# The last two expert blocks of a mixture of experts: rows returned through HBM against rows returned by products with slot matrices

## The chip, the cores and the metric

One core of one Trainium2 chip. The metric is the device time of one execution in microseconds (us), lower is better. The engines named are TensorE (PE), VectorE (DVE), ScalarE (ACT), GpSimd (POOL) and SyncE (SP), which issues transfers.

## The reference, cut to what matters

Two network blocks run over 256 tokens of 1024 elements in float32. The first has two layers of feed-forward and mixer stages, the second a recurrent and attention mixer and then a mixture of 16 experts with two experts for each token. Only the end of the second is touched:

```python
combine = einsum('nk,nke->ne', w_sel, one_hot(e_id, 16))   # two weights for each token
for e in range(16):
    he = silu(hf @ w1[e]) * (hf @ w3[e])                   # 1024 -> 512
    y = y + combine[:, e:e + 1] * (he @ w2[e])             # 512 -> 1024
x = x + g2[:, None, :] * y
```

## The kernel before

All weights are streamed from HBM in units of 128x2048 float32 (1 MB). Each unit is split into a high part by ScalarE (line 982) and a low part by VectorE (line 1346), and a product is made from three float32r products. In the expert stage each token is given two slots, one for each of its experts. A block is 128 slots of one expert. There are 19 blocks, 16 and three more for experts with over 128 tokens. A block takes six units: four for the two input products (`product`, lines 791 to 793) and two for the output product (`outputs`, lines 820 to 822). The order in which TensorE works in round b is: the first half of block b's input products, the transposes of block b - 1's hidden rows (`turn_hidden`, line 802), the second half of the input products, the output products of block b - 1. Gathers of the slots of the next pair of blocks (`gather`, line 775) lie between them; they use one-hot matrices that POOL makes (`one_hot`, lines 553 and 556).

Each engine has its own queue, written out by hand, and waits on semaphores. Of a block's output rows ScalarE evicts the left 512 columns from bank 3 (line 1041, semaphore `y_left`) and VectorE the right 512 from bank 4, multiplied by the gain in `mod` (line 1504, semaphore `y_right`). The output products of a block wait for both evictions of the block before it, and for hTlo (line 1484), which VectorE makes after ScalarE's hThi (line 1028). The rows go to `ybuf`, which is the tile that the profile names lnrow, and POOL stores them in the HBM tensor `yd` (`store`, line 564). After block 18 POOL waits for the last two stores and issues four indirect reads (line 577): for each half of the tokens (i) and each choice (j), 128 rows of 4 KB from `yd` to `raw`. ScalarE weights the first choice (line 1046), VectorE adds the second, weighted (line 1510), multiplies the left half by the gain (line 1514) and adds the sum to x (line 1516). SP sends four pieces of x out (line 506).

The 1 MB tiles for loaded units are six: three thirds of `raw`, two parts of `mod`, and `raw5`. SP loads the next unit into a tile when the low split of the unit in it is done.

Of the kernel before, what the change touches and what calls it, by code (L numbers as in the profile page):

```python
# [68 lines left out]
D_EXPERT = 512  # L69
V_SC, V_RC, V_RCB, V_BM, V_RGB, V_A, NVEC = 0, 3, 7, 8, 10, 12, 13  # L70
# [108 lines left out]
def build(nc, t, out):  # L179
    ctx = ExitStack()  # L180
    with ctx:
# [48 lines left out]
        def xT_banks(i):  # L230
# [103 lines left out]
        tests = sb("tests", [P, 2, BATCH], F32, moe)  # L334
        oneh = sb("oneh", [P, 2, TT, BATCH], F32R, moe)
# [76 lines left out]
            "hT_ps y_left y_right first_w final").split()}  # L412
# [69 lines left out]
        def sp_block2(sp):  # L482
            for p in range(6 * BLOCKS):
                b, j = UNIT_OF[p]
                if p < RING:
                    sp.wait_ge(lo_done, UNITS - (UNITS - 1 - p) % RING + RING)
                elif p == 3:
                    sp.wait_ge(ev["h1_free"], 1)
                elif p == 4:
                    sp.wait_ge(x_done, 4 * N_H2 + 4)  # L490
                elif p >= RAWS:
                    unit_split(sp, p - RAWS)
                if p == 0:
                    expert = 0
                elif j == 0:
                    if b == 1:
                        sp.wait_ge(ev["emap"], 1)
                    expert, last = sp.value_load(emap[0:1, b:b + 1], min_val=0, max_val=EXPERTS - 1), expert
                e = expert if j < 4 or b == BLOCKS - 1 else last
                src = t["experts"][bass.ds(e * 6 + j, 1), :, :]  # L500
                sp.dma_start(raws[p % RAWS], src.rearrange("o p n -> p (o n)")).then_inc(expert_loaded(p)[0], 16)
            for i in range(TT):
                for half in range(2):
                    cs = slice(512 * half, 512 * half + 512)
                    sp.wait_ge(ev["final"], 2 * i + half + 1)
                    sp.dma_start(out[0, i * P:(i + 1) * P, cs], x[:, i, cs]).then_inc(out_done, 16)
            sp.wait_ge(out_done, 16 * 2 * TT)

        def pool_block2(pool):
# [55 lines left out]

            pool.wait_ge(ev["slots"], 1)
            one_hot(1)
            one_hot(2)
            for b in range(BLOCKS):
                if b % 2 == 1 and b // 2 + 3 < BATCHES:  # L570
                    one_hot(b // 2 + 3)
                store(b)
            for b in (BLOCKS - 2, BLOCKS - 1):
                pool.wait_ge(stored[b % 2], stored_to(b))
            for i in range(TT):
                for j in range(2):
                    pool.indirect_dma_start(raw[:, i, j * D:(j + 1) * D], None, t["yd"],
                                            bass.IndirectOffsetOnAxis(slot_i[:, i, j:j + 1], 0)).then_inc(back[i], 16)

        def pe_block2(pe, cols_unit, tokens_unit, rows_unit, transpose_x, open_sums):  # L580
# [243 lines left out]

            for group in range(8):
                gather(0, group)
            for b in range(BLOCKS + 1):
                nxt = b // 2 + 1
                groups = [4 * (b % 2) + n for n in range(4)] if nxt < BATCHES else []
                if b < BLOCKS:  # L830
# [6 lines left out]
                    product(b, 1)  # L837
                if b >= 1:
                    turn_hidden(b - 1)
# [7 lines left out]
                if b >= 1:  # L847
                    outputs(b - 1, 4)
                    outputs(b - 1, 5)

        def act_block2(act, turn, split_xT, silu, hid_hi):
# [162 lines left out]
            for b in range(BLOCKS + 1):  # L1014
                nxt = b // 2 + 1
                pairs = [2 * (b % 2) + n for n in range(2)] if nxt < BATCHES else []
                if b < BLOCKS:
# [5 lines left out]
                    freed(b, 1)  # L1023
                if b >= 1:
# [11 lines left out]
                if b >= 1:  # L1036
# [6 lines left out]
            act.wait_ge(ev["weighed"], 1)  # L1043
            for i in range(TT):
                act.wait_ge(back[i], 32)
                act_fn(lnrow[:, i, :], raw[:, i, 0:D], ACT.Identity, scale=rt[:, i, 33:34]).then_inc(ev["first_w"], 1)

        def dve_block2(dve, pieces, turn, split_xT, hid_lo, refine):
# [388 lines left out]
            v.tensor_copy(slot_i[:, :, :], slot[:, :, :]).then_inc(ev["slots"], 1)  # L1437
# [37 lines left out]

            for b in range(BLOCKS + 1):
                nxt = b // 2 + 1
                pairs = [2 * (b % 2) + n for n in range(2)] if nxt < BATCHES else []
                if b < BLOCKS:
                    freed(b, 0)  # L1480
                    freed(b, 1)
                if b >= 1:
# [4 lines left out]
                if b < BLOCKS:  # L1487
# [9 lines left out]
                    for pair in pairs[1:]:  # L1497
                        select(nxt, pair)
                if b >= 1:
                    freed(b - 1, 4)  # L1500
                    dve.wait_ge(*expert_used(expert_unit(b - 1, 5) + 1))
                    if b >= 3:
                        dve.wait_ge(stored[(b - 1) % 2], stored_to(b - 3))
                    v.tensor_tensor(ybuf[:, (b - 1) % 2, 512:], bank(4), row(mod, 5)[:, 512:], ALU.mult).then_inc(ev["y_right"], 1)
                    freed(b - 1, 5)
            for i in range(TT):
                dve.wait_ge(ev["first_w"], i + 1)
                for half in range(2):
                    cs = slice(512 * half, 512 * half + 512)
                    v.scalar_tensor_tensor(lnrow[:, i, cs], raw[:, i, D + 512 * half:D + 512 * half + 512], rt[:, i, 34:35],  # L1510
                                           lnrow[:, i, cs], ALU.mult, ALU.add)
                    dve.drain()
                    if half == 0:
                        v.tensor_tensor(lnrow[:, i, cs], lnrow[:, i, cs], row(mod, 5)[:, cs], ALU.mult)
                        dve.drain()
                    v.tensor_tensor(x[:, i, cs], x[:, i, cs], lnrow[:, i, cs], ALU.add).then_inc(ev["final"], 1)
# [678 lines left out]
```

## Time and profile before

| | |
|---|---|
| median of 3 runs | 1994.21 us (1993.26 to 1995.16) |
| the profiled execution | 1990.22 us, span 1988.5 us |
| busy share of the span | TensorE 92%, its weight loads 85%, VectorE 70%, ScalarE 48%, POOL 8% |
| mean granted TensorE clock | 0.958 of 2.4 GHz |
| expert stage | from about 1593 us to the end; a round takes 18.7 us |

The span runs from the first to the last instruction. The busy shares are averages over all stages; the end of the span, after TensorE's last product, has to be read by itself. The chain of waits is followed back from the last instruction. In a timeline, the brackets hold how long the engine was idle before the instruction and which instruction released it.

### The profile page before, as it was taken

How to read it: one execution, taken by the hardware profiler on the slowest of the kernel's cores; microseconds unless marked ns; L12 is line 12 of the kernel's file. 1: busy time of each engine (PE TensorE's matmuls, PEld its weight loads, DVE VectorE, ACT ScalarE, POOL GpSimd, SP SyncE). 2: the span in 40 equal slices, each digit the busy share in tenths (PEclk: the TensorE clock that was granted, in tenths of full speed). 3: DMA queues.
4: the chain of work that ended last, by engine and by line, in shares of the span. 5: the costliest groups of instructions: out<-in, count | busy, mean ns of one | idle time of the engine just before them, and what ended most of it. 6: DMA issues, size and time to landing. Idle time of an engine off the chain costs nothing.

```text
span 1988.5 us, 31309 instructions
## 1 busy us (share of the span) xinstructions
PE 1830.8 (92%) x12367; PEld 1691.0 (85%) x12367; DVE 1383.9 (70%) x1417; ACT 951.6 (48%) x870; POOL 162.9 (8%) x153
## 2 busy tenths in 40 slices
PE   7999899998999899989999899988996489999995
PEld 7999799997999799979999799967984378888884
DVE  6444686856766644467785676675787678988885
ACT  4343466534433444436563433443344257777773
POOL 1000000000000000000000000010000043424401
PEclk9999899999999899989999999998997789999998
DMA  6555355653866455544556476743340279999993
GB/s 237 190 190 190 128 200 181 220 184 142 290 245 243 157 181 181 187 157 171 180 202 221 148 261 248 270 152 135 108 149 1 72 281 360 357 367 361 364 367 134
DMA packets 61893, 418.10 MB, mean 210 GB/s; under 512 B 7312, under 2 KB 7680, under 8 KB 13936
## 3 DMA queue, kind: packets, MB, share of 16 engines
q1 hardware_dynamic: 51392, 369.19, 51.8%
q0 software_dynamic: 10400, 47.73, 6.9%
q8 instruction: 58, 0.95, 0.2%
q14 instruction: 27, 0.22, 0.0%
q10 hardware_dynamic: 16, 0.01, 0.0%
HBM read 405.88 MB, written 11.02 MB: 210 GB/s over the span
## 4 chain that ended last, share of the span: by engine, by line
PE 85%; DVE 6%; issue 4%; DVEq 3%; DMA 1%; POOL 1%; POOLq 1%; ACT 0%; ACTq 0%
PE ps L1599 16%; PE ps L1600 16%; PE ps L1601 16%; PE ps L1626 5%; PE ps L1627 5%; PE ps L1630 4%; PE ps L792 3%; PE ps L791 3%; PE ps L793 3%; PE ps L820 2%; PE ps L775 2%; PE ps L821 2%; PE ps L822 2%; PE ps L1612 1%; PE ps L1613 1%
## 5 line engine op out<-in xcount | busy, mean ns | idle before, releaser
L1884 DVE TENSOR_TENSOR wlo<-raw,whi 128x2048 fp32r<-128x2048 f32 x236 | 538.1, 2291 | 343.6 <-ACT whi L1733 340.8
L1599 PE MATMUL ps<-xThi,whi 128*128 128x256 f32 x2400 | 684.9, 285 | 10.9 <-DVE xTlo L1895 8.3
L1600 PE MATMUL ps<-xTlo,whi 128*128 128x256 f32 x2400 | 683.4, 285 | 0.0
L1601 PE MATMUL ps<-xThi,wlo 128*128 128x256 f32 x2400 | 683.1, 285 | 0.0
L1733 ACT ACTIVATE whi<-raw 128x2048 fp32r<-128x2048 f32 x236 | 449.9, 1910 | 370.4 <-PE ps L1601 270.0
L1599 PEld LDWEIGHTS ps<-xThi,whi 128*128 128x128 f32 x2400 | 465.0, 194 | 15.2 <-issue 11.3
L1600 PEld LDWEIGHTS ps<-xTlo,whi 128*128 128x128 f32 x2400 | 465.0, 194 | 1.8 <-issue 0.2
L1601 PEld LDWEIGHTS ps<-xThi,wlo 128*128 128x128 f32 x2400 | 465.0, 194 | 0.0
L1346 DVE TENSOR_TENSOR wlo<-raw,whi 128x2048 fp32r<-128x2048 f32 x76 | 176.4, 2330 | 24.8 <-ACT whi L982 24.8
L982 ACT ACTIVATE whi<-raw 128x2048 fp32r<-128x2048 f32 x76 | 145.6, 1918 | 49.8 <-PE ps L793 27.4
L1627 PE MATMUL ps<-wlo,hhi 128*128 128x512 f32 x352 | 137.5, 391 | 0.0
L1626 PE MATMUL ps<-whi,hhi 128*128 128x512 f32 x352 | 137.4, 390 | 0.0
L791 PE MATMUL ps<-whi,xsel_hi 128*128 128x512 f32 x304 | 120.2, 395 | 0.8 <-ACT xsel_hi L1010 0.8
L792 PE MATMUL ps<-wlo,xsel_hi 128*128 128x512 f32 x304 | 120.2, 395 | 0.0
L793 PE MATMUL ps<-whi,xsel_lo 128*128 128x512 f32 x304 | 119.5, 393 | 0.0
L1630 PE MATMUL ps<-whi,hlo 128*128 128x512 f32 x352 | 108.5, 389 | 0.0
L1750 ACT ACTIVATE sil<-ps 128x512 f32<-128x512 f32 x44 | 26.3, 598 | 160.0 <-PE ps L1601 160.0
L1346 DVE TENSOR_TENSOR wlo<-mod,whi 128x2048 fp32r<-128x2048 f32 x38 | 88.2, 2320 | 18.9 <-ACT whi L982 18.9
L553 POOL TENSOR_SCALAR tests<-iota,slot 128x256 f32<-128x256 f32 (+1 forms) x36 | 83.1, 2310 | 49.5 <-DVE slot_i L1437 46.3
L982 ACT ACTIVATE whi<-mod 128x2048 fp32r<-128x2048 f32 x38 | 72.7, 1913 | 17.7 <-PE ps L793 17.7
L1950 DVE SCALAR_TENSOR_TENSOR mod<-adaraw,csil_now,mod 128x512 f32 (+1 forms) x96 | 72.2, 752 | 12.1 <-issue 6.5
L1630 PEld LDWEIGHTS ps<-whi,hlo 128*128 128x128 f32 x352 | 66.1, 188 | 14.1
(433 smaller groups left out, 2650.5 us busy)
## 6 DMA issues: line engine op xcount, KB each, us to landing
raw<-stream SPq DMA_DIRECT2D x236, 1024.0 KB, 4.9
raw<-experts SPq DMA_DIRECT2D x76, 1024.0 KB, 7.7
mod<-experts SPq DMA_DIRECT2D x38, 1024.0 KB, 7.2
adaraw<-ada POOLq DMA_DIRECT2D x24, 1024.0 KB, 5.2
yd<-lnrow POOLq DMA_DIRECT2D x19, 512.0 KB, 8.6
lnrow<-ln_g POOLq DMA_DIRECT2D x6, 512.0 KB, 5.1
lnrow<-ln_b POOLq DMA_DIRECT2D x6, 512.0 KB, 6.3
x_sb<-x SPq DMA_DIRECT2D x1, 1024.0 KB, 5.8
```

Of the source, the lines that this page charges most:

```text
L791: mm(o, h, wh[:, rs], start=k == 0, stop=False)
L792: mm(o, h, wl[:, rs], start=False, stop=False)
L982: act_fn(splits[p % SPLITS][0], raws[p % RAWS], ACT.Copy).then_inc(hi_done, 1)
L1346: v.tensor_tensor(splits[p % SPLITS][1], raws[p % RAWS], splits[p % SPLITS][0].bitcast(F32), ALU.subtract).then_inc(lo_done, 1)
L1599: nc.tensor.matmul(outs[tile], wh, xh[:, k, :], start=k == 0, stop=False)
L1600: nc.tensor.matmul(outs[tile], wh, xl[:, k, :], start=False, stop=False)
L1601: last = nc.tensor.matmul(outs[tile], wl, xh[:, k, :], start=False, stop=k == KD - 1)
L1626: nc.tensor.matmul(o, h, whi[:, slot, c:c + 512], start=start and k == 0, stop=False)
L1627: nc.tensor.matmul(o, h, wlo[:, slot, c:c + 512], start=False, stop=False)
L1630: last = nc.tensor.matmul(bank(4 + 2 * i + n), lo, whi[:, slot, c:c + 512], start=False, stop=stop and k == 1)
L1733: act_fn(whi[:, slot, :], raw[:, slot, :], ACT.Copy).then_inc(hi_done, 1)
L1884: v.tensor_tensor(wlo[:, slot, :], raw[:, slot, :], whi[:, slot, :].bitcast(F32), ALU.subtract).then_inc(lo_done, 1)
```

## The change

The last two blocks (17 and 18, `FAR` = 17) are no longer stored. For them VectorE builds, in round 17, matrices that hold for each token its weight at its slot (`far_shares`). TensorE transposes them in round 18 (`turn_shares`), ScalarE copies them to `share`, and after the last output product TensorE multiplies them with the rows in `ybuf` (`far_products`: four float32 products of 512 columns for each of the two blocks, in four banks). The left halves of these blocks' rows are multiplied by the gain on VectorE: block 17's in place, block 18's at its eviction. VectorE then adds the four banks to x.

The blocks 0 to 16 are stored and read as before, but the reads follow block 16's store on POOL, and the low split of unit 109, which frees the tile. A token whose slot is in the last two blocks reads a row of zeros that POOL writes ahead (`slot_i` is bounded to that row). ScalarE weights the first choice in round 18, ahead of the eviction of block 17's left half. VectorE does three of the four sums (`near_sum`) before it evicts block 18 and the fourth after it. The sums build up in the third part of `raw`.

```diff
+FAR = BLOCKS - 2
+FAR_SLOT = FAR * SLOTS
+FAR_BANKS = [5, 6, 7, 0]
...
# POOL
+            g.memset(tests[0:1, :, :], 0.0)
+            pool.drain()
+            for half in range(2):
+                pool.dma_start(t["yd"][FAR_SLOT:FAR_SLOT + 1, 512 * half:512 * half + 512],
+                               tests[0:1, :, :].rearrange("p a s -> p (a s)")).then_inc(ev["zero_row"], 16)
+            pool.wait_ge(ev["zero_row"], 32)
             pool.wait_ge(ev["slots"], 1)
...
-                store(b)
-            for b in (BLOCKS - 2, BLOCKS - 1):
+                if b < FAR:
+                    store(b)
+            unit_split(pool, expert_unit(BLOCKS - 1, 3))
+            for b in (FAR - 2, FAR - 1):
                 pool.wait_ge(stored[b % 2], stored_to(b))
...
# TensorE
+            def turn_shares():
+                pe.wait_ge(ev["shares_in"], 1)
+                for n in range(2):
+                    for i in range(TT):
+                        last = nc.tensor.transpose(bank(5, (2 * n + i) * P, (2 * n + i + 1) * P),
+                                                   tests[:, i, n * SLOTS:(n + 1) * SLOTS], eye[:, :])
+                last.then_inc(ev["shareT_ps"], 1)
+
+            def far_products(b):
+                n = b - FAR
+                for half in range(2):
+                    pe.wait_ge(ev["y_right"], FAR + 2 + (1 + half if n else 0))
+                    for i in range(TT):
+                        ins = mm(bank(FAR_BANKS[2 * half + i]), share[:, n, i, :], ybuf[:, b % 2, 512 * half:512 * half + 512],
+                                 start=n == 0, stop=n == 1)
+                        if n == 1:
+                            ins.then_inc(ev["far_ps"], 1)
...
                     product(b, 1)
+                    if b == BLOCKS - 1:
+                        turn_shares()
...
+            pe.wait_ge(ev["shareT"], 1)
+            far_products(FAR)
+            far_products(FAR + 1)
...
# ScalarE
                     freed(b, 1)
+                    if b == BLOCKS - 1:
+                        act.wait_ge(ev["shareT_ps"], 1)
+                        act_fn(share[:, :, :, :].rearrange("p n i s -> p (n i s)"), bank(5), ACT.Copy).then_inc(ev["shareT"], 1)
...
-                if b >= 1:
+                if b == BLOCKS - 1:
+                    act.wait_ge(ev["weighed"], 1)
+                    unit_split(act, expert_unit(FAR, 4))
+                    for i in range(TT):
+                        act.wait_ge(back[i], 32)
+                        act_fn(raw[:, 2, i * D:(i + 1) * D], raw[:, i, 0:D], ACT.Identity,
+                               scale=rt[:, i, 33:34]).then_inc(ev["first_w"], 1)
+                if 1 <= b < BLOCKS:
                     freed(b - 1, 4)
...
# VectorE
-            v.tensor_copy(slot_i[:, :, :], slot[:, :, :]).then_inc(ev["slots"], 1)
+            v.tensor_scalar(far[:, :, :], slot[:, :, :], float(FAR_SLOT), None, ALU.subtract)
+            v.tensor_scalar(slot_i[:, :, :], slot[:, :, :], float(FAR_SLOT), None, ALU.min).then_inc(ev["slots"], 1)
...
+            def far_shares():
+                dve.wait_ge(ev["oneh"], BATCHES - 1)
+                other = share[:, :, :, :].rearrange("p n i s -> p n (i s)")
+                for i in range(TT):
+                    v.tensor_scalar(tests[:, i, :], iota[:, :], far[:, i, 0:1], rt[:, i, 33:34], ALU.is_equal, ALU.mult)
+                    v.tensor_scalar(other[:, i, :], iota[:, :], far[:, i, 1:2], rt[:, i, 34:35], ALU.is_equal, ALU.mult)
+                dve.drain()
+                for i in range(TT):
+                    ins = v.tensor_tensor(tests[:, i, :], tests[:, i, :], other[:, i, :], ALU.add)
+                ins.then_inc(ev["shares_in"], 1)
...
+                if b == FAR:
+                    far_shares()
                 if b >= 1:
                     dve.wait_ge(hhi_done, FFN_DONE + b)
...
+                if b == BLOCKS:
+                    dve.wait_ge(ev["y_left"], FAR + 1)
+                    v.tensor_tensor(ybuf[:, FAR % 2, 0:512], ybuf[:, FAR % 2, 0:512], row(mod, 5)[:, 0:512],
+                                    ALU.mult).then_inc(ev["y_right"], 1)
+                    near_sum(0, 0)
+                    near_sum(0, 1)
+                    near_sum(1, 1)
                 if b >= 1:
...
+                    if b == BLOCKS:
+                        v.tensor_tensor(ybuf[:, (b - 1) % 2, 0:512], bank(3), row(mod, 5)[:, 0:512], ALU.mult).then_inc(
+                            ev["y_right"], 1)
                     v.tensor_tensor(ybuf[:, (b - 1) % 2, 512:], bank(4), row(mod, 5)[:, 512:], ALU.mult).then_inc(ev["y_right"], 1)
...
+            near_sum(1, 0)
+            dve.drain()
+            for half in range(2):
+                cs = slice(512 * half, 512 * half + 512)
+                for i in range(TT):
+                    n = 2 * half + i
+                    dve.wait_ge(ev["far_ps"], n + 1)
+                    v.tensor_tensor(x[:, i, cs], x[:, i, cs], bank(FAR_BANKS[n]), ALU.add).then_inc(ev["final"], 1)
```

`near_sum(i, half)` is the body of VectorE's closing loop in the kernel before, with the sums in `raw[:, 2]` in place of lnrow and without the signal to SP. SP's output transfers now go left halves first.

## Rows read from the trace of the kernel before

**Rows 1.** The page, part 1: busy time of TensorE and the others.
```profile
PE 1830.8 (92%) x12367; PEld 1691.0 (85%) x12367; DVE 1383.9 (70%) x1417; ACT 951.6 (48%) x870; POOL 162.9 (8%) x153
```

**Rows 2.** The chain that ended last, 1958 to the end: start, duration, what.
```profile
1959.22 0.70 DVE hTlo L1484
1960.01 0.47 PE ps L820
...
1965.51 0.24 PE ps L822
...
1967.01 2.90 DMA yd<-lnrow
...
1970.74 1.04 POOL raw L577
1972.08 5.40 DMA raw<-yd,slot_i
1977.57 1.16 ACT lnrow L1046
...
1985.40 0.69 DVE x_sb L1516
```

**Rows 3.** Timeline of TensorE, modulation stage: start, duration, line, form, count.
```profile
1332.64 3.60 PE L586 MATMUL ps<-mod,ones 128*128 128x512 f32 x8
```

**Rows 4.** Timeline of VectorE, 1932 to the end.
```profile
1932.72 0.68 DVE L1484 TENSOR_TENSOR hTlo<-ps,hThi 128x512 fp32r<-128x512 f32 x1
...
1939.13 0.42 DVE L1459 CAST xsel_lo<-ps 128x256 fp32r<-128x256 f32 x1
...
1943.72 4.55 DVE L1346 TENSOR_TENSOR wlo<-raw,whi 128x2048 fp32r<-128x2048 f32 x2 [0.32 <-ACT whi L982]
...
1978.75 0.75 DVE L1510 SCALAR_TENSOR_TENSOR lnrow<-raw,rt,lnrow 128x512 f32<-128x512 f32 x1 [12.28 <-ACT lnrow L1046]
...
1980.96 0.75 DVE L1510 SCALAR_TENSOR_TENSOR lnrow<-raw,rt,lnrow 128x512 f32<-128x512 f32 x1
...
1982.39 0.74 DVE L1510 SCALAR_TENSOR_TENSOR lnrow<-raw,rt,lnrow 128x512 f32<-128x512 f32 x1
```

**Rows 5.** Groups by form of VectorE, from 1560: busy time, mean ns, idle before.
```profile
L1439 DVE TENSOR_SCALAR mod<-iota,slot 128x256 f32<-128x256 f32 x2 | 0.8, 456 | 0.0
```

**Rows 6.** Timeline of TensorE, rounds 17 and 18.
```profile
1935.49 0.45 PE L820 MATMUL ps<-whi,hThi 128*128 128x512 f32 x1
...
1941.01 0.39 PE L791 MATMUL ps<-whi,xsel_hi 128*128 128x512 f32 x1
...
1946.51 0.60 PE L802 MATMUL ps<-eye,mod 128*128 128x128 f32 x4
```

**Rows 7.** Timeline of ScalarE, round 18: eviction of block 17's left half.
```profile
1958.10 0.60 ACT L1041 ACTIVATE lnrow<-ps 128x512 f32<-128x512 f32 x1 [3.52 <-PE ps L822]
```

**Rows 8.** DMA issues of 1940 to 1945 and of 1900 to 1990, us to landing.
```profile
yd<-lnrow POOLq DMA_DIRECT2D x1, 512.0 KB, 4.0
...
raw<-yd,slot_i POOLq DMA_INDIRECT x4, 5.4
```

**Rows 9.** Timeline of POOL, the last stores and the last read.
```profile
1943.94 0.53 POOL L564 DMA_DIRECT2D yd<-lnrow  x1 [18.17 <-DVE lnrow L1504]
...
1967.01 0.53 POOL L564 DMA_DIRECT2D yd<-lnrow  x1 [7.14 <-DVE lnrow L1504]
...
1974.61 0.94 POOL L577 DMA_INDIRECT raw<-yd,slot_i  x1 [0.30 <-issue]
```

**Rows 10.** Instructions on the tile tests, POOL: shortest, median, longest in ns.
```profile
L553 POOL TENSOR_SCALAR tests<-iota,slot x36: 1137/2432/5103, 1591.4 to 1880.9; 128x256 f32<-128x256 f32 x32, 128x128 f32<-128x128 f32 x4
```

**Rows 11.** Timeline of TensorE, round 1: the gathers that wait for POOL.
```profile
1611.21 1.22 PE L775 MATMUL ps<-oneh,xThi 128*128 128x256 f32 x4 [4.98 <-POOL oneh L556]
```

**Rows 12.** Stretches of 1 us: busy of each engine, granted clock (PEclk), DMA share.
```profile
1609.00:1610.00 1.00, 0.00 (x0) 0.00 (x0) 1.00 (x1) 0.14 (x1) 1.00 (x1) 0.54 1.25 377
...
1615.00:1616.00 1.00, 1.00 (x3) 0.78 (x3) 0.00 (x0) 0.00 (x0) 0.85 (x2) 0.55 1.18 238
```

More of the change, by code:

```diff
@@ L334, in build @@
         tests = sb("tests", [P, 2, BATCH], F32, moe)
+        far = sb("far", [P, TT, 2], F32, moe)
+        share = sb("share", [P, 2, TT, SLOTS], F32, moe)
         oneh = sb("oneh", [P, 2, TT, BATCH], F32R, moe)
@@ L411, in build @@
             "tables_in h2_hi h2_lo picked rank_ps emap slots weighed oneh0 oneh "
-            "hT_ps y_left y_right first_w final").split()}
+            "hT_ps y_left y_right first_w final zero_row shares_in shareT_ps shareT far_ps").split()}
         out_done = sem("out_done")
@@ L501, in sp_block2 @@
                 sp.dma_start(raws[p % RAWS], src.rearrange("o p n -> p (o n)")).then_inc(expert_loaded(p)[0], 16)
-            for i in range(TT):
-                for half in range(2):
+            for half in range(2):
+                for i in range(TT):
                     cs = slice(512 * half, 512 * half + 512)
-                    sp.wait_ge(ev["final"], 2 * i + half + 1)
+                    sp.wait_ge(ev["final"], 2 * half + i + 1)
                     sp.dma_start(out[0, i * P:(i + 1) * P, cs], x[:, i, cs]).then_inc(out_done, 16)
@@ L576, in pool_block2 @@
                 for j in range(2):
[L577 removed]
+                    pool.indirect_dma_start(raw[:, i, j * D:(j + 1) * D], None, t["yd"][0:FAR_SLOT + 1, :],
                                             bass.IndirectOffsetOnAxis(slot_i[:, i, j:j + 1], 0)).then_inc(back[i], 16)
@@ L1042, in act_block2 @@
                     freed(b - 1, 5)
[L1043 to L1046, printed above, removed]
         def dve_block2(dve, pieces, turn, split_xT, hid_lo, refine):
@@ L1474, in dve_block2, with near_sum @@
             v.tensor_tensor(R(33, 35), R(33, 35), R(3, 4).to_broadcast([P, TT, 2]), ALU.mult).then_inc(ev["weighed"], 1)
+            def far_shares():
[8 more added lines that the diff above has]
+                ins.then_inc(ev["shares_in"], 1)
+            def near_sum(i, half):
+                dve.wait_ge(ev["first_w"], i + 1)
+                cs = slice(512 * half, 512 * half + 512)
+                acc = raw[:, 2, i * D + 512 * half:i * D + 512 * half + 512]
+                v.scalar_tensor_tensor(acc, raw[:, i, D + 512 * half:D + 512 * half + 512], rt[:, i, 34:35], acc,
+                                       ALU.mult, ALU.add)
+                dve.drain()
+                if half == 0:
+                    v.tensor_tensor(acc, acc, row(mod, 5)[:, cs], ALU.mult)
+                    dve.drain()
+                v.tensor_tensor(x[:, i, cs], x[:, i, cs], acc, ALU.add)
             for b in range(BLOCKS + 1):
@@ L1503, in dve_block2 @@
                         dve.wait_ge(stored[(b - 1) % 2], stored_to(b - 3))
+                    if b == BLOCKS:
+                        v.tensor_tensor(ybuf[:, (b - 1) % 2, 0:512], bank(3), row(mod, 5)[:, 0:512], ALU.mult).then_inc(
+                            ev["y_right"], 1)
                     v.tensor_tensor(ybuf[:, (b - 1) % 2, 512:], bank(4), row(mod, 5)[:, 512:], ALU.mult).then_inc(ev["y_right"], 1)
                     freed(b - 1, 5)
[L1506 to L1516, printed above, removed]
+            near_sum(1, 0)
+            dve.drain()
+            for half in range(2):
+                cs = slice(512 * half, 512 * half + 512)
+                for i in range(TT):
+                    n = 2 * half + i
+                    dve.wait_ge(ev["far_ps"], n + 1)
+                    v.tensor_tensor(x[:, i, cs], x[:, i, cs], bank(FAR_BANKS[n]), ALU.add).then_inc(ev["final"], 1)
         def proj_bank(name, a):
```

## The prediction

> **What bounds the kernel now.** I read the page first: TensorE is busy for 92% of the span [rows 1], so only what shortens its stream or the stretches without it can pay. Then the chain of waits, in its last stretch [rows 2]. TensorE's last product of the last expert block starts at 1965.51 us and ends at about 1965.74. From there to the end of the span, at 1988.5, TensorE does nothing: 22.8 us. The chain in that tail is serial: eviction, store of block 18 to HBM (2.90 us), the first two of four indirect reads (issued from 1970.74, landed at 1972.08 + 5.40 = 1977.48), ScalarE's weighting of 1.16 us at 1977.57, VectorE's sums until 1986.09, then the output transfer. The reader is to see that every link waits for the one ahead, and that no engine is busy twice. The change works on this tail. The question is what it puts in its place and what it pushes into the stream in front.
>
> **The new tail, from the end T of the last product.** TensorE goes on with eight products of a float32 share matrix and a block's rows. The nearest rows are the four float32 products of 512 columns in the modulation stage: 8 records (two for each product) in 3.60 us, the first seven of them 3.0 us apart, so 0.43 us a record and 0.86 us a product [rows 3]. Four for block 17 need only rows that are there; four for block 18 need VectorE's two evictions, ready 1.4 us after T, inside the first four. So TensorE sets the pace: 8 x 0.86 = 6.9 us, 0.2 us for the last one's drain through the array and the semaphore, and the last addition starts at T + 7.1. In the kernel before, the last addition starts at 1985.40 and the span ends at 1988.5, 3.1 us later, and that part stays [rows 2]. Since the next product can start some 0.1 us before the modelled end of the last, the new tail is 10.1 us. Saved: 22.8 - 10.1 = 12.7 us. At half clock the eight products would take 13.7 us; I exclude that for the likeliest case, as TensorE comes straight from 24 products.
>
> VectorE's own work must not come later. In its last round it now does one gain product, and three of the four sums, beside the last 24 products. Its rows are 2.21 us for a sum with the gain (1978.75 to 1980.96) and 1.43 us without (to 1982.39) [rows 4], with 0.6 for the gain product 5.7 us in all. The 24 products take 1960.01 to 1965.74, 5.7 us [rows 2]. That just fits. The fourth sum, 2.2 us, lies under the share products. Only when the reads land late do these three come late, and the same wait then holds TensorE, below.
>
> **What is added ahead, on VectorE.** The share matrices are built in round 17 between the weight splits and the product hTlo of block 16: four compares of 128x256 and two additions. The nearest row is the compare at 0.456 us [rows 5]; overlapped, some 0.4 each, 2.4 us in all. hTlo starts at 1932.72 [rows 4] and would now end at 1935.8; TensorE wants it at 1935.49 [rows 6]. That costs 0.4 to 0.5 us. The queue behind it is also later: the selection at 1939.13 [rows 4] comes some 2 us later, to 1941.5, where TensorE wants it at 1941.01 [rows 6] (0.5 later by now). Together 0.6 us; bounds 0 (all in VectorE's gaps) and 2.4. Two splits later VectorE is back in step. The loads that SP issues behind these splits move by up to 2 us, and their landings lie 5 us ahead of use.
>
> **On TensorE** four transposes go between the products of block 18. The same form, four of them, stands at 1946.51: the four records span 0.60 us, of which the last's drain of some 0.2 us overlaps the next product [rows 6]. I take 0.4; the bounds are 0.3 and 0.6. So the end of block 17's outputs moves from 1957.9 to 1958.9, and with the transposes of block 18's hidden rows TensorE has nothing to do from 1959.3.
>
> **On ScalarE** the copy of the shares, 0.6 us, lies in its gap: it idles for 3.52 us before 1958.10 [rows 7]. Removed are the stores of blocks 17 and 18 (POOL's queue, 0.5 us each, nobody waited for the first). The row of zeros is written by POOL while it waits for the slots; the extra small instruction ahead of the slots' semaphore delays POOL and the first gathers by some 0.1 us (below the 0.46 us of the wide compare, as it has 4 columns).
>
> **The moved reads and the new wait.** POOL issues the reads after the store of block 16. That store is issued at 1943.94 and lands after 4.0 us [rows 8, 9]; with VectorE's eviction about 0.9 later (the delay above, less the gap before it), it lands at 1948.9. POOL then takes 0.8 to 1.1 us to wake, so the first read is issued at 1950.0. Loads of weights are over by then. In the kernel before, the four were issued from 1970.74 to 1974.61, each landing 4.2 to 5.5 us after its issue, the median 5.4 [rows 2, 8, 9]; so the first pair is in after 6.7 us and the second after 9.3. Moved: 1956.7 and 1959.3.
>
> Who waits? ScalarE, whose queue now has the two weightings before the eviction of block 17's left half. Behind that stands hThi of block 18, then VectorE's hTlo, then TensorE's last 24 products, which need all of them. In the kernel before the chain is eviction 1958.10 [rows 7], hThi 0.5 later, hTlo 1959.22, product 1960.01 [rows 2]. Now the second weighting starts at 1959.4 and takes 1.15, the eviction starts at 1960.6, hThi at 1961.1, hTlo at 1961.7, and the products at 1962.5. Without the reads they would start at 1961.0. The reads cost 1.5 us.
>
> Sum: 12.7 saved, less 0.6, 0.4, 0.1 and 1.5, gives 10.1 us. The profiled execution took 1990.22 us at a span of 1988.5; the median of the runs shown is 4 us (0.2%) above it. 1994.2 - 10.1 = **1984.1 us**. About 0.2%, 4 us, is what a measurement can tell from no change.
>
> **Reads that start beside VectorE's splits.** In the kernel before the reads ran with VectorE idle. Now they are issued beside VectorE's last three splits, some 2.3 us each (the two from 1943.72 took 4.55 [rows 4]). What POOL does beside such splits is seen in two rows: its compares take 1.14 us at best and 2.43 us at the median, 5.10 at most [rows 10]; but its plain transfer, issued at 1943.94 inside a double split, took 0.53 us, as it did at 1967.01 with VectorE idle [rows 9]. The read is nearer to the second, so I take no delay; the other end is 1.3 us for each of four reads.
>
> On this, the Trainium skill speaks against the change: SBUF — State Buffer holds, under the shared port pair, that a GpSimd instruction which reads SBUF and a VectorE instruction with two SBUF inputs exclude each other, and that descriptors of transfers issued from GpSimd starve when it is locked out. The compares agree with that rule and the plain transfer does not show it; by it the result would be that of the second rival.
>
> **Rivals.**
> First, **the reads are hidden**: they need to land by 1957.9, 1.5 us earlier than worked out. For it: the store alone took 2.90 us [rows 2], and 1.1 of its 4.0 is the load beside it. Against: that load moves later too. It gives 1982.6, and with the share matrices fully in VectorE's gaps 1982.0.
>
> Second, **POOL held off by the splits**: 1.3 us for each read, 5.2 in all. TensorE's products start at 1967.7, after 8.4 us of idleness. The clock then matters: before 1611.21 TensorE had idled 4.98 us [rows 11], the granted clock had fallen to half (1.2 GHz) in the stretch from 1609, and it was back at full (2.4 GHz) only in that from 1615 [rows 12], 4.3 us of work later; half of this, 2.2 us, is lost. Sum: 10.1 - 5.2 - 2.2 = 2.7 us, 1991.5. A partial delay of 1 to 3 us gives 1985 to 1987.
>
> Third, **slower, by the same queue**: the decision is in one landing. If each read is held as long as POOL's longest compare (5.10 instead of 1.14), the second pair lands 16 us late, at 1975; the products start at 1978, and with the clock the saving turns into 10.1 - 16 - 2.2 = -8.1 us, 2002. It decides from a landing 8 us later than worked out (10.1 less the clock's 2.2), 1967.3. Against it: VectorE has only three splits left, 7 us of work, so more than 7 us of delay by it isn't to be had.
>
> Fourth, **no change that can be told**: the tail is shortened, but the share products run at half clock and the round ahead takes 2.4 us instead of 0.6: 10.1 - 6.8 - 1.8 = 1.5 us, 1992.7. Needs a long stall in front, so it joins the second.
>
> **How the numbers follow.** Likeliest case (stall of 0 to 3 us more or less as worked out): 0.55. Hidden: 0.18. Held off by about the second rival's price: 0.19 (half of it within 4 us of before). No change otherwise: 0.05. Slower: 0.03. Faster by over 0.2%: 0.55 + 0.18 + 0.09 + 0.01 = 0.83; same 0.13; slower 0.04. The range: low end the hidden case less 1.6 us for VectorE's splits or the first gathers falling more luckily (POOL's one-hot there holds TensorE 4.98 us [rows 11]), 1980.5; the high end is short of the second rival's full price, 1990.5.
>
> **What will show it.** In the tail eight float32 products of 0.86 us, the last addition about 7 us after the last expert product, and the end some 10 us after it. TensorE's idle time before the last 24 products, 1.5 us before, should be 3.2, released through hTlo. ScalarE's two weightings should lie at 1956.8 and 1959.5, each released by the read. In round 17 TensorE should wait less than 1 us for VectorE. POOL's read instructions should stay near 1 us; if they take 2 or more, the second rival holds. The prediction is wrong if the reads land after 1962 or if the granted clock falls before the last 24 products.

## The result, and the profile after

The changed kernel takes 1979.8 us (median of 4, 1978.66 to 1980.68) against 1994.33 us (median of 4); the ratio is 0.993 with a 95% interval of [0.9917, 0.9942]. It is faster, as forecast (1984.1 us), but 14.5 us less where 10.1 were forecast, and 0.7 us outside the stated range. The two profiled executions differ less: 1990.22 us before and 1980.68 after, 9.5 us. Two numbers that differ this much need a clock of their own, so I first measure both traces from one event that lies ahead of everything that the change touches in the expert stage, TensorE's first gather. Timelines of TensorE, after:

```profile
1594.92 1.23 PE L790 MATMUL ps<-oneh,xThi 128*128 128x256 f32 x4 [4.55 <-DVE oneh L1489]
...
1602.42 0.47 PE L806 MATMUL ps<-whi,xsel_hi 128*128 128x512 f32 x1 [0.83 <-ACT xsel_hi L1050]
```

Before, the same gather starts at 1593.00 us. From there to the end of the span it is 1988.5 - 1593.0 = 395.5 us before and 1979.0 - 1594.9 = 384.1 us after. So the change is worth **11.4 us** behind the first gather, and the changed kernel's profiled execution was 1.9 us later on arriving there. The reader is also to see what is missing in the rows: the next wait of the kernel before, 4.98 us for POOL's one-hot matrix [rows 11], is not there any more. POOL's timeline, after, shows why:

```profile
1547.06 0.51 POOL L573 MEMSET tests<- 1x512 f32 x1
1559.18 1.01 POOL L576 DMA_DIRECT2D yd<-tests  x2 [11.60 <-issue]
1593.55 2.47 POOL L559 TENSOR_SCALAR tests<-iota,slot 128x256 f32<-128x256 f32 x2 [33.35 <-DVE slot_i L1484]
1596.34 0.72 POOL L562 TENSOR_TENSOR oneh<-tests 128x256 fp32r<-128x256 f32 x1 [0.32 <-issue]
```

and the same place before:

```profile
1591.37 2.58 POOL L553 TENSOR_SCALAR tests<-iota,slot 128x256 f32<-128x256 f32 x2 [46.30 <-DVE slot_i L1437]
1600.01 0.72 POOL L556 TENSOR_TENSOR oneh<-tests 128x256 fp32r<-128x256 f32 x1 [6.05 <-issue]
```

Before, POOL stood still for 6.05 us between its compares and its first addition, and nothing that the profile names ended it ("issue"). After, that pause is 0.32 us, and a long one (11.60 us) stands behind the memset of the row of zeros, in a stretch in which POOL waits for the slots anyway.

At the other end, the chain that ended last, after:

```profile
1951.89 5.80 DMA raw<-yd,slot_i
...
1957.71 0.02 ACT raw L1084
...
1957.89 1.45 ACTq L185
1959.34 0.50 ACT hThi L1071
...
1959.86 0.70 DVE hTlo L1560
...
1960.65 0.76 PE ps L835
...
1968.69 0.23 PE ps L837
1968.93 6.88 PE ps L855 x16
...
1975.83 0.69 DVE x_sb L1599
```

It answers to [rows 2]. The serial tail of store, reads and sums is gone: behind the last expert product come the eight share products (16 records, 6.88 us) and one addition. But the chain now reaches TensorE's last 24 products through the fourth read, ScalarE's weighting and the eviction behind it. TensorE, after:

```profile
1954.61 0.60 PE L817 MATMUL ps<-eye,mod 128*128 128x128 f32 x4
1960.65 0.76 PE L835 MATMUL ps<-whi,hThi 128*128 128x512 f32 x1 [5.45 <-DVE hTlo L1560]
...
1965.48 0.63 PE L837 MATMUL ps<-whi,hTlo 128*128 128x512 f32 x1
...
1968.53 0.40 PE L837 MATMUL ps<-whi,hTlo 128*128 128x512 f32 x1
```

It idles 5.45 us, where the kernel before idled 1.5, and the first half of the 24 products takes 0.63 us for each record instead of 0.40. The granted clock in stretches (PEclk, the third number from the end) says the same:

```profile
1956.00:1958.00 2.00, 0.00 (x0) 0.00 (x0) 0.00 (x0) 0.29 (x1) 0.00 (x0) 1.00 0.46 188
1958.00:1960.00 2.00, 0.00 (x0) 0.00 (x0) 0.14 (x1) 1.83 (x3) 0.00 (x0) 0.80 0.00 0
1960.00:1962.00 2.00, 1.35 (x3) 1.16 (x4) 1.93 (x4) 0.00 (x0) 0.00 (x0) 0.50 0.00 0
...
1966.00:1968.00 2.00, 2.00 (x10) 1.65 (x9) 0.21 (x1) 0.00 (x0) 0.00 (x0) 0.99 0.00 0
```

It fell to half (1.2 GHz) within 1958 to 1960, while TensorE waited, and was back at 2.4 GHz by 1966. Why the reads came late is seen in two timelines, POOL's and VectorE's, after:

```profile
1944.95 1.03 POOL L592 DMA_INDIRECT raw<-yd,slot_i  x1 [4.14 <-DVE wlo L1392]
1946.29 2.18 POOL L592 DMA_INDIRECT raw<-yd,slot_i  x1 [0.30 <-issue]
1948.78 2.81 POOL L592 DMA_INDIRECT raw<-yd,slot_i  x1 [0.31 <-issue]
1951.89 2.50 POOL L592 DMA_INDIRECT raw<-yd,slot_i  x1 [0.30 <-issue]
```

```profile
1945.33 2.29 DVE L1392 TENSOR_TENSOR wlo<-mod,whi 128x2048 fp32r<-128x2048 f32 x1 [0.94 <-ACT whi L1022]
...
1948.48 2.29 DVE L1392 TENSOR_TENSOR wlo<-mod,whi 128x2048 fp32r<-128x2048 f32 x1 [0.26 <-ACT whi L1022]
...
1951.29 2.28 DVE L1392 TENSOR_TENSOR wlo<-raw,whi 128x2048 fp32r<-128x2048 f32 x1
```

The first read was issued in VectorE's gap before a split and took 1.03 us. Each of the other three meets a split. The splits end at 1947.62, 1950.77 and 1953.57; the reads end at 1948.47, 1951.59 and 1954.39, each 0.82 to 0.85 us behind a split's end. That is a read that starts its work only when the split is over. The Trainium skill (SBUF — State Buffer, Who interferes with whom) states such a mutual exclusion of a VectorE instruction with two SBUF inputs and a GpSimd instruction that reads SBUF. This trace agrees for the reads that began under a split, 2.18 to 2.81 us for 1.03. It does not show the reverse: the split that began under the first read took its usual 2.29 us.

The account, position by position on both traces:

```
                                      before     after    after - before
first gather starts                  1593.00   1594.92    +1.92
transposes of block 0's hidden rows  1626.37   1620.92    -5.45   = 1.92 - 7.37 (POOL's pause)
transposes of block 16's hidden rows 1927.81   1923.55    -4.26   = -5.45 + 1.19 (rounds 2 to 17)
transposes of block 18's hidden rows 1957.90   1954.61    -3.29   = -4.26 + 0.97 (rounds 17, 18)
last 24 products start               1960.01   1960.65    +0.64   = -3.29 + 3.93 (reads)
last of them starts                  1965.35   1968.53    +3.18   = +0.64 + 2.54 (half clock)
end of the span                      1988.5    1979.0     -9.5    = +3.18 - 12.7 (tail)
```

The 7.37 us lie between the first gather and the transposes of round 1: 33.4 us before and 26.0 us after. In the changed kernel without the drain, below, it is 33.5 us again, so the 7.37 us are the pause and the half clock behind it. The 1.19 us that are lost later belong to no step of the change that I can name. The 24 output products of a round take 5.59 us where they took 5.47. Two lines of the profile between 1640 and 1900 us show it, the output products of hThi before and after (shortest, median and longest in ns):

```profile
L820 PE MATMUL ps<-whi,hThi x107: 389/389/404, 1653.0 to 1899.5; 128*128 128x512 f32 x107
```

```profile
L835 PE MATMUL ps<-whi,hThi x112: 393/396/396, 1647.7 to 1898.5; 128*128 128x512 f32 x112
```

That makes two rounds 37.84 us long where they were 37.70, at full granted clock in both. All profiles of the changed kernel and its variants have it, the one without the memset and the drain too; the kernel before with a drain does not. Why it is so stays open: no run varied it.

Of the 0.97 us in rounds 17 and 18, by TensorE's timelines, 0.15 is the wait for hTlo, 0.07 lies ahead of the share transposes, 0.43 is these, and two times 0.16 are the slower output products again.

### The profile page after: what moved, and what is told of

Read it like the earlier page. It is cut to its first block, busy times and chain, and to the rows that moved or that the text cites. A ratio compares the mean times of both kernels' runs of the same rounds, so it can differ in the third digit from the quotient of the medians.

```text
span 1979.0 us, 31365 instructions
## 1 busy us (share of the span) xinstructions
PE 1843.0 (93%) x12387; PEld 1696.8 (86%) x12387; DVE 1388.8 (70%) x1430; ACT 950.9 (48%) x870; POOL 171.5 (9%) x154
## 4 chain that ended last, share of the span: by engine, by line
PE 86%; DVE 7%; DVEq 3%; issue 1%; ACT 1%; DMA 1%; POOL 1%; POOLq 0%; ACTq 0%
PE ps L1682 16%; PE ps L1684 16%; PE ps L1683 16%; PE ps L1709 5%; PE ps L1710 5%; PE ps L1713 5%; PE ps L806 3%; PE ps L807 3%; PE ps L808 3%; PE ps L790 2%; PE ps L835 2%; PE ps L836 2%; PE ps L837 2%; PE ps L1695 1%; PE ps L1696 1%
## 5 line engine op out<-in xcount | busy, mean ns | idle before, releaser
L559 POOL TENSOR_SCALAR tests<-iota,slot 128x256 f32<-128x256 f32 (+1 forms) x36 | 82.8, 2302 | 37.7 <-DVE slot_i L1484 33.4
L1664 POOL DMA_DIRECT2D adaraw<-ada x24 | 12.7, 528 | 794.8 <-DVE tick L2036 441.4
```

## The experiments

Eight variants ran beside the changed kernel, and the kernel before once more. Each is timed against the kernel before on the same chip; the column "from the gather" is the span's end less the start of the first gather in the run's profile.

```
                    median us  ratio [95%]               from the gather
changed kernel        1979.8   0.993  [0.9917, 0.9942]   384.1
POOL memset + drain   1985.0   0.9956 [0.9939, 0.9973]   387.7
POOL drain only       1985.14  0.996  [0.9948, 0.9972]   388.4
no memset, no drain   1988.86  0.9982 [0.9969, 0.9995]   391.4
late weightings       1974.65  0.9908 [0.9891, 0.9924]   377.8
reads wait            1986.73  0.9963 [0.9951, 0.9976]   388.9
plain reads           1975.31  0.9914 [0.9896, 0.9932]   377.7
splits from PSUM      1976.85  0.9906 [0.9888, 0.9925]   380.5
early share products  1972.25  0.9902 [0.9883, 0.992]    376.4
before, once more     1987.41  (one execution)           395.4
```

The last column has a scatter of its own of up to 0.7 us. In the first gather TensorE works at half clock for a while, and in the profiles of "POOL memset + drain" and "early share products" the granted clock came back 1 to 2 us sooner than in the others. By the transposes of round 1 these two were at 25.4 and 25.3 us from the gather, the drain alone and the changed kernel at 26.0. Smaller differences between two rows are to be read position by position. The ratios of the late weightings, the plain reads, the splits from PSUM and the early share products have overlapping intervals, so their times alone do not put these four in an order.

### POOL's pause

**Memset and drain in the kernel before.**

```diff
+            g.memset(tests[0:1, :, :], 0.0)
+            pool.drain()
             pool.wait_ge(ev["slots"], 1)
```

> The kernel before with one memset of 2 KB and one drain on POOL ahead of its wait for the slots, and nothing else of the change. Theory (a pause that POOL takes once, at its first computing instructions of the stage, is moved under an idle stretch): POOL's idle time of 6.05 us before its first addition goes to under 0.5 us, TensorE's wait of 4.98 us for the one-hot matrix and the half clock behind it are gone, 5 to 6.5 us saved, about 1988.5 us. Rival (the pause differs from execution to execution, or the gain of the changed kernel in this stretch comes from its transfers of zeros): no change, 1994.3 us.

Measured: 7.8 us less from the gather. POOL's timeline:

```profile
1592.79 2.48 POOL L553 TENSOR_SCALAR tests<-iota,slot 128x256 f32<-128x256 f32 x2 [46.62 <-DVE slot_i L1439]
1595.42 0.73 POOL L556 TENSOR_TENSOR oneh<-tests 128x256 fp32r<-128x256 f32 x1 [0.15 <-issue]
```

The pause is 0.15 us and TensorE's wait for POOL is gone from its list of waits. Two instructions that compute nothing of use are worth more than half of what the whole change brought.

**The changed kernel without them.** The zeros come from a tile that is zero already.

```diff
-            g.memset(tests[0:1, :, :], 0.0)
-            pool.drain()
-            for half in range(2):
-                pool.dma_start(t["yd"][FAR_SLOT:FAR_SLOT + 1, 512 * half:512 * half + 512], ...)
-            pool.wait_ge(ev["zero_row"], 32)
+            pool.dma_start(t["yd"][FAR_SLOT:FAR_SLOT + 1, :].rearrange("o (p n) -> (o p) n", n=P),
+                           zero_w[0:KD, :].bitcast(F32)).then_inc(ev["zero_row"], 16)
+            pool.wait_ge(ev["zero_row"], 16)
```

> The changed kernel with the row of zeros taken from a tile that is zero already, so without the memset and the drain on POOL. Theory of the pause: it is back ahead of POOL's first addition, TensorE waits about 5 us for the one-hot matrix, 1985 to 1986 us. Rival (the transfers, or a few instructions more or less in POOL's stream, moved the pause): as the changed kernel, 1979.8 us.

Measured: the pause is back with nearly the length of before, and TensorE waits for it (POOL, then TensorE):

```profile
1602.64 0.73 POOL L562 TENSOR_TENSOR oneh<-tests 128x256 fp32r<-128x256 f32 x1 [6.13 <-issue]
```

```profile
1613.85 1.22 PE L787 MATMUL ps<-oneh,xThi 128*128 128x256 f32 x4 [5.16 <-POOL oneh L562]
```

From the gather it is 391.4 us, 7.3 more than the changed kernel. The transfers of zeros are not what moved the pause.

**The drain alone, in the kernel before.**

```diff
+            pool.drain()
             pool.wait_ge(ev["slots"], 1)
```

> The kernel before with one drain on POOL ahead of its wait for the slots, and no memset. If POOL's pause belongs to its first drain behind a row of transfers, it is taken under the idle stretch: no pause ahead of the first addition, 7 us less than before, about 1986 us. If it belongs to its first computing instruction, the pause stays, 1993 us.

Measured: 388.4 us from the gather, 7.1 less than before, and again 0.15 us ahead of the first addition. So the pause belongs to POOL's first drain behind its row of transfers, not to its first computing instruction.

### The reads

**The reads held until the last split is done.**

```diff
-            unit_split(pool, expert_unit(BLOCKS - 1, 3))
+            unit_split(pool, expert_unit(BLOCKS - 1, 5))
```

> The changed kernel with POOL's four reads held until the last low split (unit 113) is done. Theory (the reads take 2.2 to 2.8 us each because VectorE's splits shut POOL out): each read now takes 1.0 us, from 1953.7 us; the second pair lands at 1963.5 instead of 1957.7, TensorE idles 11 us, and the end comes 6 us later, about 1986 us. Rival (they are slow through the transfers under way or through their number): the reads still take 2.2 to 2.8 us each, the second pair lands at 1968 to 1969, the end comes 11 us later, about 1991 us.

Measured: the reads behind the last split, POOL's timeline:

```profile
1956.20 1.03 POOL L592 DMA_INDIRECT raw<-yd,slot_i  x1 [13.04 <-DVE wlo L1392]
1957.54 0.98 POOL L592 DMA_INDIRECT raw<-yd,slot_i  x1 [0.30 <-issue]
1958.82 0.94 POOL L592 DMA_INDIRECT raw<-yd,slot_i  x1 [0.30 <-issue]
1960.06 0.94 POOL L592 DMA_INDIRECT raw<-yd,slot_i  x1 [0.31 <-issue]
```

Full speed, as in the kernel before. TensorE idles 11.44 us before its last 24 products, 6.0 us more than in the changed kernel. The end comes only 4.8 us later (6 forecast), because the clock came back sooner: the 24 products took 7.0 us instead of 8.1. The rival, that they are slow by their number, is out; what else ran in that stretch is still open.

**Plain transfers in place of the gather by slot.** The gather by slot is left out: fixed rows of the same size are read.

```diff
-                    pool.indirect_dma_start(raw[:, i, j * D:(j + 1) * D], None, t["yd"][0:FAR_SLOT + 1, :],
-                                            bass.IndirectOffsetOnAxis(slot_i[:, i, j:j + 1], 0)).then_inc(back[i], 16)
+                    pool.dma_start(raw[:, i, j * D:(j + 1) * D],
+                                   t["yd"][(2 * i + j) * SLOTS:(2 * i + j + 1) * SLOTS, :]).then_inc(back[i], 16)
```

> The changed kernel with its four indirect reads replaced by plain transfers of 128 rows each from the same HBM tensor, issued by POOL at the same place (the gather by slot is left out). Theory (an indirect read has to read its column of indices in SBUF and is shut out by VectorE's two-input splits, a plain transfer isn't): 0.53 us for each, the second pair lands by 1951.5, TensorE waits 1.5 us before its last 24 products, full clock, about 1973.5 us. Rival (everything that POOL issues there is held): 2 to 3 us for each transfer, as the changed kernel, 1979.8 us.

Measured, POOL and VectorE:

```profile
1947.57 2.09 POOL L592 DMA_DIRECT2D raw<-yd  x4 [3.76 <-DVE wlo L1392]
```

```profile
1948.34 2.29 DVE L1392 TENSOR_TENSOR wlo<-mod,whi 128x2048 fp32r<-128x2048 f32 x1 [0.94 <-ACT whi L1022]
```

Four in 2.09 us, though a split began at 1948.34 and lay over the last two of them. TensorE idles 1.5 us, the end is at 377.7 us from the gather. A plain transfer isn't held, an indirect one is. So the starving of descriptors that the prediction named beside the exclusion is not seen here. (The landing forecast was too early: ScalarE's second weighting started at 1956.18 on a released read, 6.5 us behind the end of the issues; it no longer held anybody.)

**The last three splits with one SBUF operand.** VectorE's split of units 111 to 113 takes its first operand from PSUM. The true low parts of these three units are left out.

```diff
+                if p >= expert_unit(FAR, 5):
+                    v.tensor_tensor(splits[p % SPLITS][1].rearrange("p (a n) -> p a n", a=4),
+                                    bank(6).unsqueeze(1).to_broadcast([P, 4, 512]),
+                                    splits[p % SPLITS][0].bitcast(F32).rearrange("p (a n) -> p a n", a=4),
+                                    ALU.subtract).then_inc(lo_done, 1)
+                    return
                 v.tensor_tensor(splits[p % SPLITS][1], raws[p % RAWS], splits[p % SPLITS][0].bitcast(F32),
                                 ALU.subtract).then_inc(lo_done, 1)
```

> The changed kernel, with VectorE's last three low splits (units 111 to 113) taking their first operand from a PSUM bank instead of the SBUF tile raw: same shape and engine, one SBUF operand instead of two (these three units' low parts are left out of the result). Theory (POOL's reads are shut out by a VectorE instruction with two SBUF operands, whatever else runs): the splits still take about 2.3 us, the four reads take 0.94 to 1.04 us each, the second pair lands 5.4 us after its issue, TensorE waits 1.5 us before its last 24 products and runs at full clock, about 6.3 us less than the changed kernel, from the first gather to the end 377.8 us instead of 384.1. Rival (a busy VectorE, or the other work of that stretch, slows the reads): they still take 2.2 to 2.8 us, 384.1 us.

Measured, VectorE and POOL:

```profile
1947.66 2.29 DVE L1393 TENSOR_TENSOR wlo<-ps,whi 128x2048 fp32r<-128x2048 f32 x1 [0.94 <-ACT whi L1022]
```

```profile
1947.22 1.03 POOL L592 DMA_INDIRECT raw<-yd,slot_i  x1 [4.08 <-DVE wlo L1398]
1948.56 0.98 POOL L592 DMA_INDIRECT raw<-yd,slot_i  x1 [0.31 <-issue]
1949.84 0.94 POOL L592 DMA_INDIRECT raw<-yd,slot_i  x1 [0.30 <-issue]
1951.09 0.94 POOL L592 DMA_INDIRECT raw<-yd,slot_i  x1 [0.31 <-issue]
```

VectorE is exactly as busy as before, the reads take 0.94 to 1.03 us. Of the four reads two lie wholly inside a split. That settles the cause: it is the second SBUF operand of the split. The time, however, was not what I expected. TensorE idled 2.7 us and not 1.5, because ScalarE's second weighting, released at 1957.30, still stands ahead of the eviction (the prediction had this right, with 3.2). And the clock fell although TensorE had been at work again for more than 1 us (stretches of 1 us; PEclk is the third number from the end):

```profile
1960.00:1961.00 1.00, 0.76 (x3) 0.68 (x4) 1.00 (x3) 0.00 (x0) 0.00 (x0) 1.00 0.00 0
1961.00:1962.00 1.00, 1.00 (x5) 0.80 (x4) 0.93 (x2) 0.00 (x0) 0.00 (x0) 0.78 0.06 16
1962.00:1963.00 1.00, 1.00 (x4) 0.81 (x3) 0.93 (x3) 0.00 (x0) 0.00 (x0) 0.50 0.00 0
```

So 3.6 us came back, from the gather, of the 6.3 expected.

**The weightings moved behind hThi.** On ScalarE they no longer stand ahead of the eviction.

```diff
                     act_fn(hThi[:, :, :].rearrange("p f s -> p (f s)"), bank(2), ACT.Copy).then_inc(hhi_done, 1)
+                if b == BLOCKS:
+                    (the two weightings)
...
-                if b == BLOCKS - 1:
-                    (the two weightings)
                 if 1 <= b < BLOCKS:
```

> The changed kernel with ScalarE's two weightings behind hThi of block 18 instead of ahead of the eviction of block 17. Theory (TensorE's 5.45 us of idleness and the half clock come from this queue): TensorE idles about 1.6 us before the last 24 products, they run at full clock, the last product ends at 1962.4 us on the changed kernel's time line, the end comes 6.4 us earlier, about 1973.4 us. Rival (VectorE's sums become the bound, since the second pair of rows lands at 1957.7 and VectorE is held beside the evictions): 2 to 3 us of it are given back, about 1976 us.

Measured: 377.8 us from the gather, 6.3 less than the changed kernel. POOL's reads are as slow as ever (1.95 to 2.81 us for the last three), but only the weightings wait for them. TensorE, then VectorE:

```profile
1956.38 0.47 PE L835 MATMUL ps<-whi,hThi 128*128 128x512 f32 x1 [1.51 <-DVE hTlo L1560]
...
1962.04 7.03 PE L855 MATMUL ps<-lnrow,share 128*128 128x512 f32 x16
```

```profile
1962.24 0.69 DVE L1588 TENSOR_TENSOR lnrow<-ps,mod 128x512 f32<-128x512 f32 x1 [0.32 <-PE ps L837]
```

TensorE idles 1.51 us again and goes at full clock; VectorE even waits 0.32 us for the last product with its three sums done, so the rival (VectorE as the bound) is out for this version. In the changed kernel the cost comes of both, the place of the weightings in ScalarE's queue and the held reads. With plain reads the wait is 1.5 us too, with indirect reads that are not held it is 2.7, and behind hThi they may be slow at no cost.

**Two share products ahead of the last 24**, on top of it.

```diff
-            def far_products(b):
+            def far_products(b, half):
...
+                if b == BLOCKS:
+                    pe.wait_ge(ev["shareT"], 1)
+                    far_products(FAR, 1)
                 if b >= 1:
                     outputs(b - 1, 4)
                     outputs(b - 1, 5)
-            pe.wait_ge(ev["shareT"], 1)
-            far_products(FAR)
-            far_products(FAR + 1)
+            far_products(FAR, 0)
+            far_products(FAR + 1, 0)
+            far_products(FAR + 1, 1)
```

> The kernel of the run with the late weightings, and the share products of block 17's right half put ahead of TensorE's last 24 products, where it waits for hTlo. Theory (the tail behind the last product is TensorE's float32 products, one for one): two of the eight products leave the tail, 1.7 us less there, 0.6 us of it given back because they begin only when block 17's right half is evicted and end after hTlo; about 1.1 us less than that run, 1973.5 us. Rival (VectorE's evictions and sums bound the tail): no gain, 1974.6 us.

Measured: 1.3 us less from the gather, and the lowest median, 1972.25 us at a ratio of 0.9902, though its interval overlaps that of the late weightings. Only 0.6 of the 1.3 us is the edit's: 0.7 lay between the gather and round 1, where the two kernels are the same. From the transposes of block 18's hidden rows to the end it is 17.4 us against 18.0, so 0.6 us less, where 1.1 were forecast. TensorE's timeline:

```profile
1953.82 1.96 PE L854 MATMUL ps<-lnrow,share 128*128 128x512 f32 x4 [0.44 <-DVE lnrow L1592]
...
1961.22 5.31 PE L854 MATMUL ps<-lnrow,share 128*128 128x512 f32 x12
```

The chain that ended last no longer goes through these products. Behind the last expert product it is VectorE's:

```profile
1961.42 0.69 DVE lnrow L1590
...
1964.98 1.88 DVE x_sb L1601 x3
```

VectorE's four additions run without a gap in 2.48 us. In the version before each waited 0.17 us or more for a product. So theory and rival each hold in part: with eight share products TensorE sets the pace of the tail, with six VectorE does.

### Executions of one kernel

**The kernel before, once more.**

> The kernel before once more, for a second profile, since its profiled execution (1990.22 us) lay 4 us under its median. If executions differ ahead of the expert stage, the stretch from the first gather to the end is as long as in the first profile, 395.5 us. If they differ in POOL's pause, it is not.

Measured: 1987.41 us, and 1985.6 - 1590.24 = 395.4 us from the gather, as in the first profile (395.5), with the same pause of 6.05 us. The executions differ ahead of the expert stage: over the eleven profiles of this study the first gather starts between 1590.24 and 1597.88 us. Medians of the kernel before in later comparisons were 1992.63, 1992.24 and 1993.98 us. So about 3 us of the 14.5 between the two first medians may well be of this kind. That 11.4 us are the change rests on one profile of it and two of the kernel before, with the scatter of up to 0.7 us named above; it lies just below the 11.6 us that the ratio's interval allows at least, and where the rest comes from I could not show.

## Why the prediction was wrong

The direction and the tail were right; a gain and two costs were missing or too small, and the largest error was in the gain.

- **The new tail (10.1 us forecast, saving 12.7).** Right. From the start of the last expert product to the end of the span it is 1979.0 - 1968.53 = 10.5 us against 1988.5 - 1965.35 = 23.2 us before, 12.7 us less. 16 records of 0.43 us, as in [rows 3]; the last addition 7.1 us behind the product's end.
- **Share matrices, transposes and copy (1.0 us forecast).** Right in kind, 0.65 us. VectorE's compares followed each other every 0.32 us and not 0.4, so hTlo came only 0.15 us late; the transposes took 0.43.
- **The output products.** The sum has no term for them. They lost 1.5 us over rounds 2 to 18, by the account above, and the cause is open.
- **POOL's preamble ("the extra small instruction ahead of the slots' semaphore delays POOL and the first gathers by some 0.1 us").** Wrong step, the one that decided. I costed the row of zeros at nothing, because POOL waits there anyway, and looked only at what its instructions add. The drain behind the memset takes over a pause of 6 us that stood unexplained in the trace, in the round of [rows 11]. Its removal is worth 7.4 us by the account, 7.1 to 7.8 us when put into the kernel before by itself, 7.3 us when taken out of the changed one. Of a kernel that differs from before by 11.4 us, 7 come from a drain. I named that round only as a place where something might fall "more luckily", at 1.6 us.
- **The reads ("The read is nearer to the second, so I take no delay").** Wrong step. A plain transfer was the wrong neighbour: it isn't held (0.53 us, four in 2.09 us over the splits), an indirect one is (2.18 to 2.81 us). The cost on TensorE was 3.9 us of waiting and 2.5 us of half clock, 6.5 us where 1.5 was taken. This is the second rival, given 0.19: its mechanism held, at 5.0 us beyond the forecast's 1.5 where it had 7.4. Two of the prediction's own signs of being wrong came with it: reads of 2 us or more, and a granted clock that fell before the last 24 products. That every stall of the read lay in ScalarE's queue ahead of the eviction was right, and moving the weightings returned 6.3 us.
- **The sum.** 12.7 + 7.4 - 1.5 - 0.65 - 6.5 = 11.4 us, where the forecast had 12.7 - 0.6 - 0.4 - 0.1 - 1.5 = 10.1. A gain of 7.4 us that was not in the sum and costs of 5.0 and 1.5 us that were not in it either nearly cancelled. That the sum came so close was luck. The rest up to 14.5 us may be the scatter of executions ahead of the stage, which I could not show; my range took none of it, though the profiled execution stood 4 us under its median.

Open: what POOL does in the pause. The drain is shown to be its place. In the kernel before, POOL's last transfer of the row was issued at 1544.54 us and landed 9.0 us later, by the trace's list of DMA issues, some 40 us ahead of the pause; so that the drain waits for transfers in flight is no explanation there. It does fit the pauses behind the later stores, which all these kernels have. In the kernel before there are seven of them, of 0.95 to 4.55 us, and each ends 0.17 to 0.24 us after the store ahead of it has landed: the store issued at 1680.32 us lands after 9.7 us, at 1690.02, and POOL's addition starts at 1690.26. No run varied these, so that they are waits for the store is read from the traces and not tested.

## What to carry to other kernels

An "issue" pause of several microseconds on an engine that others wait for is a term of its own: find the instruction at which it stands, and try whether one drain in an idle stretch takes it away, before anything larger is built. An indirect read issued by POOL should be priced beside what VectorE runs then, not beside a plain transfer; and whatever waits for such a read belongs at the end of its engine's queue, behind everything that TensorE needs. When two errors of a forecast can cancel, compare positions in the two traces from a common event, not totals.

## What the runs showed of the hardware

- POOL's first drain behind a row of transfers paused it 6.05 us, in both profiles of the kernel before, some 40 us after the last of them had landed; one drain earlier left 0.15 us. The drains behind later stores ended 0.17 to 0.24 us after the store had landed (seven of seven in the kernel before).
- An indirect read took 0.94 to 1.04 us alone, beside a split with one PSUM operand, or when it had begun ahead of the split. It took 1.95 to 2.81 us when it began under a split with two SBUF operands, and ended 0.81 to 0.85 us behind it. A plain transfer took 0.53 us under such a split as with VectorE idle.
- The granted clock of TensorE fell to half in an idle stretch of 5.45 us, and in one profile after an idle stretch of 2.7 us, when TensorE had been at work again for more than 1 us; idle stretches of 1.5 us at the same place left it at 2.4 GHz. The fall cost 2.5 us in the first case and 1.5 us in the second (24 products in 7.2 us, for 5.7 with the weightings moved).
- A float32 product of 512 columns took two records of 0.43 us at full clock, 16 records in 6.88 us.
